# A recurrent layer that reads the undivided residual by halves of tokens, with the token's factor put on its outputs

## The reference, cut to what matters

```
h = h + rms_norm(sq_relu_mlp(a, w1, w2), gains)        # end of the first MLP
a = rms_norm(h, gains)                                 # norm_2
q_x, f_x, i_x, g_x = split(a @ w_in)                   # 8 heads, 128 columns of each per head
f = lb + (1 - lb) * sigmoid(f_x); q = silu(q_x); k = 1 - f; v = i_x
b = cumsum(log f) within chunks of 32 tokens
o = causal(q e^(b-ref) . k e^(ref-b)) v + (q e^b) state     # within a chunk, plus the carried state
state = decay * state + (k e^(last-b))^T v                  # from chunk to chunk, 16 chunks
out = (rms_norm(o, o_norm) * silu(g_x)) @ w_o
```

## Time and profile before

| | us |
|---|---|
| median of 3 runs (2849.51 to 2856.66) | 2854.09 |
| profiled execution, whole | 2849.57 |
| its span, first to last instruction | 2847.7 |
| from the last matmul of the MLP tail to the first projection of the mixer (611.06 to 629.12) | 18.1 |
| from there to the first `turn_out` (703.00) | 73.9 |
| from the first to the seventh `turn_out` (703.00 to 874.35) | 171.4 |

### The profile page before, as it was taken

The page is one execution under the profiler, slowest core; times in us unless marked ns, Lnnn a source line. Parts: engine busy times, 40 slices in busy tenths (PEclk is TensorE's granted clock), DMA queues, the critical chain, the costliest instruction groups (busy, mean ns, idle before and its releaser), DMA issues.

```text
span 2847.7 us, 38919 instructions
## 1 busy us (share of the span) xinstructions
PE 2699.2 (95%) x13991; PEld 2165.7 (76%) x13991; DVE 1614.7 (57%) x3021; ACT 1136.8 (40%) x1958; POOL 122.6 (4%) x106
## 2 busy tenths in 40 slices
PE   7999999999999999998998988999999989999998
PEld 5567888887777788887775876677877768788887
DVE  6335725446765743635845357755677775564451
ACT  4444322225664322223446326842355652332221
POOL 0000000000000000000220010000011110000000
PEclk9999999999999999998999989999999999999999
DMA  3112333321222233331110220022222212333331
GB/s 141 45 59 64 109 101 96 96 67 62 79 66 82 67 111 96 97 96 60 60 60 12 93 67 9 1 67 81 82 67 74 68 60 84 117 108 98 96 96 66
DMA packets 59684, 217.83 MB, mean 76 GB/s; under 512 B 6432, under 2 KB 6560, under 8 KB 59424
## 3 DMA queue, kind: packets, MB, share of 16 engines
q1 hardware_dynamic: 57920, 209.76, 23.5%
q0 software_dynamic: 1632, 6.29, 0.6%
HBM read 211.83 MB, written 4.19 MB: 76 GB/s over the span
## 4 chain that ended last, share of the span: by engine, by line
PE 79%; DVE 10%; ACT 3%; DVEq 3%; issue 3%; ACTq 0%; DMA 0%; POOL 0%; SPq 0%
PE ps L371 23%; PE ps L372 22%; PE ps L373 22%; DVE work L2099 1%; PE ps L512 1%; DVE big L3258 1%; DVEq L3316 1%; PE ps L763 1%; DVE work L2118 1%; DVE ring_lo L311 1%; PE ps L2024 1%; ACT ring_hi L304 1%; PE ps L468 1%; PE ps L1853 1%; PE ps L573 1%
## 5 line engine op out<-in xcount | busy, mean ns | idle before, releaser
L371 PE MATMUL ps<-a_hi,ring_hi 128*128 128x512 f32 (+1 forms) x1976 | 779.1, 394 | 46.7 <-DVE ring_lo L311 23.8
L373 PE MATMUL ps<-a_hi,ring_lo 128*128 128x512 f32 (+1 forms) x1976 | 765.2, 387 | 0.0
L372 PE MATMUL ps<-a_lo,ring_hi 128*128 128x512 f32 (+1 forms) x1912 | 739.5, 387 | 0.0
L311 DVE TENSOR_TENSOR ring_lo<-ring,ring_hi 128x1024 fp32r<-128x1024 f32 x357 | 436.8, 1225 | 504.6 <-ACT ring_hi L304 474.4
L304 ACT ACTIVATE ring_hi<-ring 128x1024 fp32r<-128x1024 f32 x377 | 397.0, 1056 | 503.8 <-PE ps L373 503.3
L371 PEld LDWEIGHTS ps<-a_hi,ring_hi 128*128 128x128 f32 x1976 | 375.6, 190 | 132.1 <-DVE ring_lo L311 18.0
L373 PEld LDWEIGHTS ps<-a_hi,ring_lo 128*128 128x128 f32 x1976 | 375.4, 190 | 76.3
L372 PEld LDWEIGHTS ps<-a_lo,ring_hi 128*128 128x128 f32 x1912 | 363.4, 190 | 70.2 <-issue 1.2
L372 PE MATMUL ps<-hid_lo,ring_hi 128*128 128x512 f32 (+1 forms) x992 | 380.5, 384 | 0.0
L371 PE MATMUL ps<-hid_hi,ring_hi 128*128 128x512 f32 (+1 forms) x928 | 354.5, 382 | 0.0
L373 PE MATMUL ps<-hid_hi,ring_lo 128*128 128x512 f32 (+1 forms) x928 | 354.2, 382 | 0.0
(11 more groups left out here) (419 smaller groups left out, 3233.0 us busy)
## 6 DMA issues: line engine op xcount, KB each, us to landing
ring<-weights SPq DMA_DIRECT2D x392, 512.0 KB, 3.6
h<-x SPq DMA_DIRECT2D x1, 2048.0 KB, 9.2
residual<-h POOLq DMA_DIRECT2D x4, 512.0 KB, 3.5
h<-residual POOLq DMA_DIRECT2D x1, 2048.0 KB, 11.1
out<-h POOLq DMA_DIRECT2D x1, 2048.0 KB, 7.9
tab<-tables SPq DMA_DIRECT2D x1, 1648.0 KB, 15.4
big<-positions SPq DMA_DIRECT2D x1, 256.0 KB, 3.5
col<-columns SPq DMA_DIRECT2D x1, 164.5 KB, 3.9
```

Source lines behind the costliest of these rows:

```text
L311: dve.tensor_tensor(lo, M.ring[:, b % RING, :], hi.bitcast(F32), ALU.subtract).then_inc(M.sem("blocks_split"), 1)
L371: pe.matmul(out, w_hi, hi, start=start, stop=False)
L372: pe.matmul(out, w_hi, lo, start=False, stop=False)
L373: return pe.matmul(out, w_lo, hi, start=False, stop=stop)
```

## The change

1. **Seam.** norm_2 becomes deferred. Each tile of `h` is multiplied by its gain alone, rounded on ACT and its rest taken on DVE as soon as it is added (`open_halves_act`, `open_halves_dve`), and PE multiplies it at once (`open_halves_pe`). Sums of squares run beside; the second half's are added up on DVE (`square_sum`). The branch norm's total and spread of the first half move into the MLP's last two blocks; those of the second half stand between projection tiles.
2. **Factor on the outputs.** q, f and g are multiplied by the token's factor (`R.scale`, spread once, in `project(0)` of head 0) on DVE into SBUF (`scaled_qf`, `R.gx`), and the sigmoids read SBUF. v gets its factor per token in four pieces on ACT (`values`). `hg_qf` and `hg_gx` take the place of `hg_banks_free` and `hg_gate_free`.
3. **Order of a head.** The split of the output of head i-1 stands behind the chain of states of head i (`split_y`); `q_dec` moves into `front`; head 0 projects five eighths of v before its chunk products.
4. **Around it.** The lower bounds are computed during the attention heads; POOL splits no block of the first head, DVE does; two blocks use other slots (`split_slot`, `HOLDER`).

```diff
@@ down_tail_pe
+    if name == "mlp0":
+        block(NT - 1, 0, TILE_BANK[1], TOKENS[1], {4: lambda: total(0)}).then_inc(used, 1)
+        block(NT - 1, 1, TILE_BANK[1], TOKENS[1], {2: lambda: spread(0)}).then_inc(used, 1)
+        return lambda: total(1), lambda: spread(1)
@@ open_halves_pe (new, takes the place of input_halves_pe)
+    pe.wait_ge(M.sem("mlp0_down1_free"), NT + 3)
+    idle_pe(pe, M, 3, 2)
+    for half in range(2):
+        for k in range(NT):
+            pe.wait_ge(M.sem("norm_scaled"), NT * half + k + 1 + M.past(norm, "scaled"))
...
+            if half == 0:
+                total(k)
+                if k == 1:
+                    branch[0]()
+                if k == 4:
+                    branch[1]()
+    pe.wait_ge(M.sem("later_half_summed"), NT)
+    half_total_pe(pe, M, INPUT_BANK[0], M.ssum, 1, False, True).then_inc(M.sem("norm_total"), 1)
@@ open_halves_dve (new); added = gain, add to h; low = rest of the rounded tile
+    tile(0)
+    summed(0)
+    half_inverse_dve(dve, M, branch, 0)
+    added(0, 0)
+    rest_block(dve, M, FIRST[down] + 2 * NT + 3)
+    low(0, 0)
+    tile(1)
...
+    for k in range(NT):
+        added(1, k)
+        if k:
+            square_sum(k - 1)
+        low(1, k)
+    square_sum(NT - 1)
@@ mlp_dve
-    for n in range(2):
+    for n in range(3 if name == "mlp0" else 2):
@@ hgrn_pe
-    readers = ["hg_banks_free", "hg_banks_free", "hg_v", "hg_gate_free"]
+    readers = [("hg_qf", 2), ("hg_qf", 2), ("hg_v", 1), ("hg_gx", 1)]
...
+        elif nxt:
+            project(0, i, 1, {1: spread})
+            project(1, i, 1)
+            project(2, i, 1, ks=range(0, 5))
@@ hgrn_act
     def values(i, ahead):
-        act.activation(R.v, M.bank(2), ACT.Copy).then_inc(M.sem("hg_v"), 1)
+        for t in range(QT):
+            s = slice(t * P, (t + 1) * P)
+            copy = act.activation(R.v[:, s], M.bank(2)[:, s], ACT.Copy, scale=R.scale_col[:, t:t + 1])
...
     def front(i, ahead):
-        act.activation(R.f, M.bank(1), ACT.Sigmoid).then_inc(M.sem("hg_sig"), 1)
-        act.activation(R.sq, M.bank(0), ACT.Sigmoid).then_inc(M.sem("hg_sig"), 1)
-        act.activation(R.sg, M.bank(3), ACT.Sigmoid).then_inc(M.sem("hg_sig"), 1)
+        act.wait_ge(M.sem("hg_qf"), i * 2 + (2 * ahead + 2))
+        act.activation(R.f, R.f, ACT.Sigmoid).then_inc(M.sem("hg_sig"), 1)
+        act.activation(R.sq, R.qx, ACT.Sigmoid).then_inc(M.sem("hg_sig"), 1)
+        act.wait_ge(M.sem("hg_gx"), i + (ahead + 1))
+        act.activation(R.sg, R.gx, ACT.Sigmoid).then_inc(M.sem("hg_sig"), 1)
@@ hgrn_dve
+    def scaled_qf(i, ahead):
+        dve.wait_ge(M.sem("blocks_used"), i * 4 + (FIRST["hgrn_heads"] + 4 * ahead + 1))
+        dve.tensor_tensor(R.qx, M.bank(0), R.scale, ALU.mult).then_inc(M.sem("hg_qf"), 1)
+        dve.wait_ge(M.sem("blocks_used"), i * 4 + (FIRST["hgrn_heads"] + 4 * ahead + 2))
+        dve.tensor_tensor(R.f, M.bank(1), R.scale, ALU.mult).then_inc(M.sem("hg_qf"), 1)
     def front(i, ahead):
+        dve.wait_ge(M.sem("blocks_used"), i * 4 + (FIRST["hgrn_heads"] + 4 * (ahead + 1)))
+        dve.tensor_tensor(R.gx, M.bank(3), R.scale, ALU.mult).then_inc(M.sem("hg_gx"), 1)
...
     def body
             dve.nop().then_inc(M.sem("hg_chained"), 1)
+        if prev and nxt:
+            split_y(i - 1)
@@ pool
-            for j in (2, 3):
-                rest_block(pool, M, FIRST["hgrn_heads"] + j)
```

More of the change, by code:

```diff
@@ L1168, in total @@
     def total(half):
-        pe.wait_ge(M.sem("norm_summed"), NT + half + M.past(branch, "summed"))
+        if half and name == "mlp0":
+            pe.wait_ge(M.sem("last_half_summed"), 1)
+        else:
+            pe.wait_ge(M.sem("norm_summed"), NT + half + M.past(branch, "summed"))
         half_total_pe(pe, M, BRANCH_BANK[half], M.ssum, half).then_inc(M.sem("norm_total"), 1)
@@ L1229, in input_halves_pe, with open_halves_pe, total, part @@
             spread(1)
+LATE_TILES = 2
+def open_halves_pe(pe, M, norm, name, n, a_lo, branch):
+    def total(k):
+        pe.wait_ge(M.sem("norm_squared"), k + (k > 0) + M.past(norm, "squared"))
+        half_total_pe(pe, M, INPUT_BANK[0], M.sq[:, k % 2, :], 0, k == 0, k == NT - 1)\
+            .then_inc(M.sem("norm_summed"), 1)
+    def part(half, k, j):
+        b, cols = FIRST[name] + j, TOKENS[half]
+        if half == 0 and k == 0:
+            wait_split(pe, M, b)
+        mm = split_matmul(pe, M, M.bank(j)[:, cols], b, k, M.a_hi[:, k, cols], a_lo[:, k, cols], k == 0, k == NT - 1)
+        if half == 1 and k == NT - 1:
+            mm.then_inc(M.sem("blocks_used"), 1)
+    pe.wait_ge(M.sem("mlp0_down1_free"), NT + 3)
[3 more added lines that the diff above has]
+            pe.wait_ge(M.sem("norm_scaled"), NT * half + k + 1 + M.past(norm, "scaled"))
+            if half == 0 and k < LATE_TILES:
+                for j in range(n - 1):
+                    part(half, k, j)
+            else:
+                if half == 0 and k == LATE_TILES:
+                    for late in range(LATE_TILES):
+                        part(half, late, n - 1)
+                for j in range(n):
+                    part(half, k, j)
+            if half == 0:
[6 more added lines that the diff above has]
+    half_total_pe(pe, M, INPUT_BANK[0], M.ssum, 1, False, True).then_inc(M.sem("norm_total"), 1)
@@ new lines, in open_halves_act, with tile @@
+def open_halves_act(act, M, norm, name, gain):
+    branch = f"{name}_down"
+    def tile(half, k):
+        cols = TOKENS[half]
+        act.wait_ge(M.sem("norm_added"), NT * half + k + 1 + M.past(branch, "added"))
+        act.activation(M.a_hi[:, k, cols], M.h[:, k, cols], ACT.Copy, scale=gain(k)).then_inc(M.sem("tile_rounded"), 1)
+        if k >= 2 and half:
+            act.wait_ge(M.sem("later_half_summed"), k - 1)
+        elif k >= 2:
+            act.wait_ge(M.sem("norm_summed"), k - 1 + M.past(norm, "summed"))
+        act.activation(M.sq[:, k % 2, cols], M.h[:, k, cols], ACT.Square).then_inc(M.sem("norm_squared"), 1)
+    tile(0, 0)
+    half_square_act(act, M, name, 1)
+    for k in (1, 2):
+        tile(0, k)
+    half_branch_root_act(act, M, name, 1)
+    for k in range(3, NT):
+        tile(0, k)
+    for k in range(NT):
+        tile(1, k)
@@ L1518, in hgrn_bounds_dve @@
     dve.drain().then_inc(M.sem("small_ready"), 1)
+def hgrn_bounds_dve(dve, M, R):
+    t = [R.tmp[:, n, :] for n in range(5)]
     dve.wait_ge(M.sem("small_done"), 2)
@@ L1629, in added_states @@
             states()
+        if nxt and prev:
+            project(2, i, 1, {5: added_states})
+        elif nxt:
+            project(2, i, 1, ks=range(5, 8))
+            added_states()
         if nxt:
-            project(2, i, 1, added_states)
             project(3, i, 1)
@@ L1790, in body @@
             rest_next(i, 1, 0)
+        if prev and not nxt:
+            split_y(i - 1)
         for t in range(QT):
@@ L1815, in body @@
         dve.drain()
-        split_dve(dve, R.norm, tile_at(R.y_hi, i), tile_at(R.y_lo, i)).then_inc(M.sem("hg_y_split"), 1)
         if nxt:
-            front_rest()
-    dve.wait_ge(M.sem("blocks_split"), splits_before(FIRST["hgrn_heads"] + 4))
+            gated(i, 1)
+        else:
+            split_y(i)
+    dve.memset(R.masked, 0.0)
     rest_next(0, 0, 0)
-    front(0, 0)
-    front_rest()
-    with dve.Fori(0, 7) as i:
-        body(i, True)
-    body(7, False)
+    dve.wait_ge(M.sem("norm_root"), 1 + M.past("norm_2", "root"))
+    dve.reciprocal(R.scale_col, M.root[:, 0:QT]).then_inc(M.sem("norm_inverse"), 1)
+    dve.wait_ge(M.sem("norm_spread"), 1 + M.past("norm_2", "spread"))
+    dve.tensor_copy(R.scale, M.norm_bank("norm_2"))
+    dve.drain()
+    scaled_first()
+    rest_next(0, 0, 1)
+    front(0, 0)
+    gated(0, 0)
+    scaled_qf(0, 1)
+    body(0, False, True, True)
+    with dve.Fori(1, 6) as i:
+        body(i, True, True, True)
+    body(6, True, True, False)
+    body(7, True, False, False)
     to_m_dve(dve, M, "hgrn_o", rest_ahead(dve, M))
```

197 lines of the change are left out of this document (141 added, 56 removed), and 4 rows, old and new, of the table NORMS.

## The result

The changed kernel's median is 2859.18 us (2857.35 to 2864.05, 10 runs), that of the kernel before 2854.05 us (2849.06 to 2857.59, 10 runs, taken on the same chip). The ratio is 1.0022 with a 95% interval of 1.0013 to 1.0031: slower by 0.22%, which lies within the 0.3% that the prediction took as no change, though the interval leaves out 1. 2859 was forecast.

A forecast was written before the change was run, and what follows sets the result against it. PE, busy 95%, bounds the kernel before; after the change the DVE and ACT ring sets the heads' period. -8.0 + 7.75 + 5.1 = +4.85 on the profiled 2849.57 gives 2854.4, as a median 2859 us; range 2846 to 2868.

The forecast's parts named there:

- Stage 1: Seam and head 0, up to the first `turn_out`: 695.0 instead of 703.00, -8.0 us, bounds -11 and -5.
- the wait on the rest of v's block: Head 0, ahead of v's projection: PE stands with nothing to do for a new 5.3 us.
- Half 0: First half of the seam's projection: paced by PE, 15.3 us, DVE keeps up, ending near 628.8.
- half 1: Second half of the seam's projection: paced by DVE at 2.05 us per tile, 15.8 in all, to 644.6.
- the fall: Head 0, behind the wait of 5.3 us: PE's clock falls and costs 1.6 us.
- Stage 2: Six periods from first to seventh `turn_out`: 179.1 us against 171.35, +7.75, before falls of the clock.
- the ring: Chain over DVE and ACT in each head: grows from 27.35 to 29.85 us, bounds 29.4 and 30.3, setting the period.
- the clock: Waits of 2.25 us ahead of `turn_out`: three of six followed by a fall at 1.7 each, +5.1, bounds 0 and +10.2.
- the second term: In each head, behind the logarithm: v's four pieces and the product ahead of the reciprocal add 0.7 us.
- Behind the heads: From the seventh `turn_out` to the end the program is as before: 0 us.
- The sum: Whole kernel: -8.0 + 7.75 + 5.1 = +4.85 us against the profiled 2849.57, giving 2854.4; median 2859, +0.17%.
- The rule of the Trainium skill: Halved clock follows an idle stretch; 2.25 us waits between dense work cost only their length: 2853.8, as the 25% clock-holds rival.

The follow-up runs named there:

- the last kernel: Changed kernel with split ahead of chain, head 0's rest earlier, scaled copy before v's pieces, reciprocal before q e^b, last-head PE wait for v: 2831.64 us, 0.9923 of before.
- the POOL kernel: Changed kernel, but POOL instead of DVE takes the rest of the first head's fourth block during the seam: 2864.26 us, 1.0030 of the kernel before.
- five constants: Changed kernel with five matmuls on constants on PE ahead of `turn_out` in the looped heads: 2849.60 us, 0.9990 of the kernel before.
- the two small terms: Two runs on the changed kernel: v copied in one piece without its factor, 1.0016; q e^b behind the reciprocal in looped heads, 1.0017 of the kernel before.

## Why the prediction was right

**Stage 1** was forecast at -8.0 and is -6.99 between the profiled executions. Counted from the start of the MLP tail it is -8.28 (95.77 us to the first `turn_out`, where it was 104.05). The first projection comes 14.39 behind that start, where 14.55 was forecast. The wait on the rest of v's block, 5.12, was forecast at 5.3, and the run that moves the rest shows it to be that rest's place.

That the steps between came out so well is in part luck. Half 0 took 16.0 us on PE, not 15.3, and half 1 took 14.1, not 15.8. The prediction let half 1 begin with both engines level and counted the sum of squares into DVE's step. The trace shows DVE at half 1's first rest (628.94) before PE came to it (630.65), and a step of 1.95 with or without that sum. In head 0 the lower clock lasted from PE's first matmul behind the wait, at 664.13, to 668.13: the 15 matmuls there took 5.5 us and not 3.4, so the fall cost 2.1 where 1.6 was taken. The chain of states started at 674.34; the forecast was 671.5, and 673.1 with the fall, for an execution that starts the tail 1.29 earlier. The prediction's own steps there add up to 671.2, not 671.5.

**Stage 2** was forecast at +7.75 for the ring and +5.1 for the clock. The ring gave 29.91 where 29.85 was forecast. The runs bear out the mechanism (split bare on the ring: 1.5 a head) and the clock (4.83 for three falls, 5.1 forecast). For the second term (v's pieces and the product, 0.7) the last kernel shows 0.66 or more, since PE's own work ends the gain. That three of six fell, as I took for want of better, wasn't known from the rows, and that it came out so is luck: it did here, in the POOL kernel and in the kernel before with the split moved, and four of six fell in the kernel with the earlier rest.

**Behind the heads** I put 0, and the profiled pair shows +5.6, in code that is the same in both but for the end of the last head. Of it 4.3 arise between 1246 and 1376 in the changed kernel (1240 to 1366 before), where PE waits for small steps and its clock falls; the granted clock is lower there (0.87 and 0.91). The changed kernel first, then the kernel before:

```profile
1245.64:1375.84 130.20, 117.47 (x562) 95.12 (x560) 62.48 (x115) 45.84 (x89) 3.17 (x4) 0.87 0.20 62
1239.69:1365.61 125.92, 112.77 (x561) 91.20 (x560) 62.61 (x115) 45.81 (x89) 3.17 (x4) 0.91 0.20 65
```

From the seventh `turn_out` to the end the profiles of the changed kernel's variants take from 1972.1 (the last kernel) and 1973.2 (five constants) over 1976.0 (the two small terms) to 1979.0; the two on the kernel before show 1977.8 and 1976.0 where it had 1973.4. That this is decided by when the stretch is reached is my reading; no run tested it.

**The sum** of medians, +5.1, agrees with +4.85 better than it had a right to, and this too is luck. Between the profiled executions the difference is 11.2. That of before lies 4.5 under its median and that of the changed kernel 1.6 above. In both of my runs of variants of the kernel before the clock fell right behind the wait of 2.10 in the seam and once more in the small steps; in the profiled execution it fell there only once, behind 621. The two runs with the split moved, then the profiled one:

```profile
617.00:620.00 3.00, 3.00 (x9) 2.46 (x10) 2.77 (x8) 0.78 (x3) 0.00 (x0) 0.50 0.45 167
617.00:620.00 3.00, 3.00 (x9) 2.46 (x10) 2.69 (x9) 0.82 (x3) 0.00 (x0) 0.50 0.54 167
622.00:628.00 6.00, 6.00 (x20) 5.19 (x20) 3.56 (x10) 0.40 (x2) 0.00 (x0) 0.50 0.00 0
```

Their first `turn_out` came at 706.86 and 707.00 instead of 703.00, 106.9 behind the tail's start where the profiled one has 104.05. Against these, stage 1 gained 11.1 and not 8.3. So a term that I put at 0 (+5.6 in this pair) and an execution of before that was faster than its median nearly cancel. How much of either is in the typical execution isn't known.

The rule of the Trainium skill weighed above ("TensorE: Matmul & The Clock Gate", Part 1) would have made the clock hold in all heads, as the prediction read it. It didn't: the granted clock fell behind waits of 2.24 to 2.28 with dense work on both sides, and didn't behind others of 2.22 to 2.28. The trace disagrees with a plain reading of the rule; the forecast was right to go by the rows.

## What to carry to other kernels

Where two engines share a ring, the place of an operation counts, not its length: the same 1.4 us split cost 1.5 a head behind the chain of states and nothing in a wait of 1.76 ahead of it. Here a wait of 2.0 to 2.3 us on TensorE was charged a second time by the clock in some heads and not in others, and waits of 1.5 weren't, so such a wait is worth removing even where it looks small. Two terms that end together can look free when each is taken away alone; they are to be tried together. And profiled executions of two kernels are to be compared stretch by stretch, from a point that both share: here 1.3 us of the difference arose ahead of the changed code and 5.6 behind it.
